# Feed-forward gate and up projections by seven block products, down projections one pair later, modulation weights in smaller pieces

## What is computed

```python
gate, up = split(rmsnorm(x, ffn_norm) @ w_gu)          # w_gu: 1024 x (2 * 2816)
x = x + (silu(gate) * up) @ w_down                     # w_down: 2816 x 1024
c_act = silu(c)
shift, scale, g = split(c_act @ ada_w[l] + ada_b[l])   # l = 0, 1: each 1024 x 3072
shift, scale = split(c_act @ kv_ada_w + kv_ada_b)      # 1024 x 2048
```

## Time and profile before

| | us |
|---|---|
| median of 3 runs | 2555.91 (2554.61 to 2556.51) |
| the profiled execution | 2559.54 |
| its span in the trace | 2557.7 |
| PE busy in the span | 2462.2 (96%) |
| DVE busy | 1272.4 (50%) |
| POOL busy | 1133.5 (44%) |
| ACT busy | 604.0 (24%) |

### The profile page before, as it was taken

One profiled execution on the slowest core, in us unless ns is written; L12 is line 12 of the kernel. 1 busy time (PEld: TensorE's weight loads), 2 busy tenths in 40 slices (PEclk: granted clock), 3 DMA queues, 4 the chain that ended last, 5 costly groups with the idle time before them and its releaser, 6 DMA issues.

```text
span 2557.7 us, 30787 instructions
## 1 busy us (share of the span) xinstructions
PE 2462.2 (96%) x12078; PEld 2040.9 (80%) x12086; DVE 1272.4 (50%) x1519; ACT 604.0 (24%) x1197; POOL 1133.5 (44%) x519
## 2 busy tenths in 40 slices
PE   6999999999999999999999989999999999999987
PEld 5787788887877888888888877888888787888876
DVE  6337555625563444435352677352524465055665
ACT  3111545512430000000000332010110123155532
POOL 5534755034033444444444434444444443555455
PEclk9999999999999999999999999999999999999998
DMA  5511000021011323232321101111111113100033
GB/s 182 162 44 50 1 1 22 13 107 42 17 42 59 132 99 131 85 136 82 148 82 50 49 26 57 42 50 50 49 49 49 41 49 129 45 26 19 25 116 115
DMA packets 45935, 170.97 MB, mean 67 GB/s; under 512 B 4590, under 2 KB 9456, under 8 KB 40456
## 3 DMA queue, kind: packets, MB, share of 16 engines
q1 hardware_dynamic: 37832, 148.52, 16.6%
q10 hardware_dynamic: 8000, 21.01, 2.4%
HBM read 156.90 MB, written 12.57 MB: 66 GB/s over the span
## 4 chain that ended last, share of the span: by engine, by line
PE 87%; DVE 8%; ACT 2%; issue 2%; POOL 1%; DMA 0%; ACTq 0%; DVEq 0%; SPq 0%; POOLq 0%
PE ps L507 24%; PE ps L508 23%; PE ps L510 23%; PE ps L667 5%; PE ps L645 4%; PE ps L655 3%; DVE h_lo L446 1%; DVE sq_sum L350 1%; PE ps L521 1%; PE ps L523 1%; PE ps L522 1%; DVE h_lo L443 1%; DVE pool_b L2359 1%; DVE rms L381 1%; DVE pool_a L2359 0%
## 5 line engine op out<-in xcount | busy, mean ns | idle before, releaser
L1192 POOL TENSOR_TENSOR split_hi<-raw,cf 128x1024 fp32r<-128x1024 f32 x198 | 385.3, 1946 | 1202.2 <-PE ps L510 1099.8
L507 PE MATMUL ps<-h_hi,split_hi 128*128 128x512 f32 x2072 | 830.6, 401 | 36.9 <-issue 9.7
L508 PE MATMUL ps<-h_lo,split_hi 128*128 128x512 f32 x2072 | 812.2, 392 | 0.0
L510 PE MATMUL ps<-h_hi,split_lo 128*128 128x512 f32 x2072 | 664.6, 392 | 0.0
L1194 POOL TENSOR_TENSOR split_lo<-raw,split_hi 128x1024 fp32r<-128x1024 f32 x198 | 557.5, 2816 | 15.5
L507 PEld LDWEIGHTS ps<-h_hi,split_hi 128*128 128x128 f32 x2072 | 392.9, 190 | 124.5 <-issue 18.5
L510 PEld LDWEIGHTS ps<-h_hi,split_lo 128*128 128x128 f32 x2072 | 391.7, 189 | 83.1
L508 PEld LDWEIGHTS ps<-h_lo,split_hi 128*128 128x128 f32 x2072 | 393.0, 190 | 77.2 <-issue 1.7
L507 PE MATMUL ps<-act_hi,split_hi 128*128 128x512 f32 x352 | 138.8, 394 | 3.9 <-DVE act_lo L2278 3.8
L508 PE MATMUL ps<-act_lo,split_hi 128*128 128x512 f32 x352 | 137.6, 391 | 0.0
L655 PE MATMUL ps<-cf,p 128*128 128x128 f32 x712 | 122.6, 277 | 7.4 <-ACT p L797 3.3
(11 more groups left out here) (321 smaller groups left out, 3541.8 us busy)
## 6 DMA issues: line engine op xcount, KB each, us to landing
raw<-in_strips SPq DMA_DIRECT2D x198, 512.0 KB, 3.5
ada_raw<-in_ada SPq DMA_DIRECT2D x32, 1024.0 KB, 5.6
xT<-in_xT SPq DMA_DIRECT2D x4, 1024.0 KB, 7.3
xT<-in_xT ACTq DMA_DIRECT2D x4, 1024.0 KB, 8.5
out_T<-out_sb SPq DMA_DIRECT2D x16, 256.0 KB, 2.2
x_spill_d<-xT ACTq DMA_DIRECT2D x1, 3584.0 KB, 9.9
xT<-x_spill_d ACTq DMA_DIRECT2D x2, 1792.0 KB, 8.6
swa_vec_d<-vbc ACTq DMA_DIRECT2D x1, 3064.0 KB, 19.2
```

The costliest lines, as they stand in the source:

```text
L507: pe.matmul(acc[:, a:b], w_hi, hi[:, a:b], start=first, stop=False)
L508: pe.matmul(acc[:, a:b], w_hi, lo[:, a:b], start=False, stop=False)
L510: mm = pe.matmul(acc[:, a:b], w_lo, hi[:, a:b], start=False, stop=last)
L1192: pool.tensor_tensor(hi, raw[:, r, :], ones[:, 0:1].to_broadcast([P, D]), ALU.mult).then_inc(hi_split, 1)
```

## The change

The first two hidden tiles stay as they were. The 20 others go in ten pairs. For a pair, the gate projection is a block matrix product: 2 hidden tiles x (4 + 4 feature tiles) times (4 + 4 feature tiles) x 2 token halves. It is done in Strassen's way (Winograd's form): seven products of four feature tiles and 512 tokens, 12 matmuls each, instead of eight. The same holds for up. Three of the seven weight blocks are quarters as they are, four are sums or differences of quarters ("form" = a block of 128 x 512 of weights, high and low). The three token-side combinations (`sum_hi`, `sum_lo`) are formed once, during the first two tiles, by DVE (`token_sums`) and ACT (`token_high`).

- POOL forms the block sums and all low parts; ACT makes the high parts (before, POOL made both). Blocks go through four half slots, `FORM_SLOT`. Each pair has 18: 7 gate, 4 down, 7 up.
- PE does a pair's gate quad, then the 8 down products of the pair before, then its up quad; the last pair does gate and up quad and then 8 down products over four hidden tiles. The first product's PSUM result is copied to SBUF by ACT (`first_product`); DVE adds the others in half-width steps to `quad_tmp` and `gated`.
- SP loads the next pair's strip 0 after the 17th block of a pair, strip 1 after the 18th.
- The modulation goes in 8 loop iterations of 8 pieces of 512 KB (128 x 1024) in 2 buffers, with one transpose and reduction each.
- Some semaphores are shared by several events, and the program is built with `dynamic_dma_scratch_size=1024`.

```diff
-HID = 4
-FFN_GROUPS = FFN_TILES // HID
-FFN_REST = FFN_TILES - HID * FFN_GROUPS
+HID = 2
+FFN_ITERS = FFN_TILES // HID - 1
...
 S_CO = S_CQ + 4
 S_FFN = S_CO + 4
-FFN_STRIPS = 3 * HID
-S_FFN_FULL = S_FFN + 3 * FFN_REST
+S_QUADS = S_FFN + 2 * HID
+QUAD_STRIPS = 6
...
+FORMS = 18
+FORM_SLOT = [0, 1, 2, 3, 0, 1, 2, 3, 0, 1, 2, 0, 1, 2, 0, 1, 2, 3]
+FORM_BEFORE = [max(q for q in range(p - FORMS, p) if FORM_SLOT[q % FORMS] == FORM_SLOT[p]) for p in range(FORMS)]
+GATE_AT, DOWN_AT, UP_AT = 0, 7, 11
+LAST_UP_AT, LAST_DOWN_AT = 7, 14
+FORM_BANK = [0, 2, 1, 0, 1, 3, 1]
+QUAD_READS = 7
...
+            def form_low(i, p, src):
+                pool.wait_ge(form_hi, FORMS * i + p + 1)
...
+            def quad_forms(i, e, at, j):
+                form_loaded(pool, i, j)
+                form_loaded(pool, i, j + 1)
+                n = 8 * i + 4 * e
+                pool.tensor_tensor(form_sums[:, :], a21, a22, ALU.add).then_inc(form_sum, 1)
+                pool.wait_ge(form_sum, n + 1)
+                pool.tensor_tensor(a21, a21, a11, ALU.subtract).then_inc(form_sum, 1)
+                for f in range(7):
+                    if f == 2:
+                        form_split(pool, i, at + 1)
+                        pool.tensor_tensor(form_sums[:, :], a11, form_sums[:, :], ALU.subtract).then_inc(form_sum, 1)
+                    if f == 4:
+                        form_split(pool, i, at + 3)
+                        pool.wait_ge(form_sum, n + 3)
+                        pool.tensor_tensor(a12, a12, form_sums[:, :], ALU.add).then_inc(form_sum, 1)
+                    form_low(i, at + f, FORM_SOURCE[f])
...
+            def ffn_pair(i):
+                quad_forms(i, 0, GATE_AT, 0)
+                down_forms(i, DOWN_AT, 2, 4)
+                quad_forms(i, 1, UP_AT, 4)
...
+            def load_quad_strip(i, j, split):
+                if isinstance(i, int) and i == 0 and j < 2:
+                    strip_split(sp, S_QUADS - 2 + j)
+                else:
+                    sp.wait_ge(form_ready, FORMS * i + split)
+                src = dram["strips"][S_QUADS + QUAD_STRIPS * i + j] if isinstance(i, int) else \
+                    dram["strips"][bass.ds(i * QUAD_STRIPS + (S_QUADS + j), 1)].rearrange("a p n -> p (a n)")
+                sp.dma_start(raw[:, j % 2, :], src).then_inc(raw_loaded[j % 2], 16)
+            def ffn_pair(i, ada):
+                load_quad_strip(i, 0, -1)
+                load_quad_strip(i, 1, 0)
+                for k in range(3) if ada else ():
+                    load_ada(i, k)
+                load_quad_strip(i, 2, GATE_AT + 6)
+                load_quad_strip(i, 3, GATE_AT + 7)
+                if ada:
+                    load_ada(i, 3)
+                load_quad_strip(i, 4, DOWN_AT + 2)
+                load_quad_strip(i, 5, DOWN_AT + 4)
+                for k in range(4, 8) if ada else ():
+                    load_ada(i, k)
...
+            def quad(i, e, at):
+                c = 6 * e
+                begin = isinstance(i, int) and i == 0 and e == 0
...
+                    if begin and f < 3:
+                        pe.wait_ge((ffn_gate, ffn_mul, ffn_gate)[f], 2)
+                    elif f < 3:
+                        pe.wait_ge(quad_read, reads + (QUAD_READS * (e - 1) + (2, 5, 7)[f]))
+                    elif f == 3:
+                        pe.wait_ge(quad_first, 2 * i + (e + 1))
+                    else:
+                        pe.wait_ge(quad_read, reads + (QUAD_READS * e + (1, 1, 3)[f - 4]))
+                    if begin and f == 1:
+                        pe.wait_ge(token_sum, 7 * 4)
+                    if begin and f == 6:
+                        pe.wait_ge(token_sum, 7 * 4 + 1)
+                    slot, w = form_at(at + f)
+                    product(pe, bank(FORM_BANK[f]), slot, [(w + k, *form_tokens[f][k]) for k in range(4)], HALF)\
...
+            def down(i):
+                for o in range(8):
+                    if o % 2 == 0:
+                        form_split(pe, i, DOWN_AT + o // 2)
+                    if o == 0:
+                        pe.wait_ge(ffn_lo, HID * i + HID)
+                    if o < 2 and isinstance(i, int):
                         pe.wait_ge(n_ffn["sem"]["root"], n_ffn["done"] + 1)
-                    elif 0 in ks:
-                        pe.wait_ge(ffn_res, o0 + o - 1)
-                    return product(pe, pair(2 + o % 2), (2 * hid + o // tiles) % 2,
-                                   [(hid * (o % tiles) + k, act_hi[:, k, :], act_lo[:, k, :]) for k in ks],
-                                   before=(lambda j: pe.wait_ge(ffn_lo, g0 + ks[j] + 1)) if o == 0 else None,
-                                   start=ks[0] == 0, stop=ks[-1] == hid - 1)
...
+            def quad_high(i, e, at, j, fs):
+                for f in fs:
+                    if f in (0, 6):
+                        form_loaded(act, i, j + (f == 6))
+                    if f in (1, 2, 4, 5):
+                        act.wait_ge(form_sum, 8 * i + (4 * e + {1: 1, 2: 3, 4: 2, 5: 4}[f]))
+                    form_high(i, at + f, FORM_SOURCE[f])
...
+            def first_product(i, e, at):
+                form_through(act, i, at)
+                if e:
+                    act.wait_ge(quad_read, 2 * QUAD_READS * i + QUAD_READS)
+                else:
+                    act.wait_ge(ffn_done, HID * i + HID)
+                act.copy(one_sum, bank(0)).then_inc(quad_first, 1)
...
+            def hidden_high(i, hi):
+                for j in range(HID):
+                    act.wait_ge(ffn_done, HID * i + (HID + j + 1))
+                    act.copy(hi[:, j, :], gated[:, j, :]).then_inc(ffn_hi, 1)
...
+            def ffn_pair(i):
+                first_product(i, 0, GATE_AT)
+                quad_high(i, 0, GATE_AT, 0, range(4, 7))
+                down_high(i, DOWN_AT, 2, range(4))
+                gate_silu(i + 1)
+                quad_high(i, 1, UP_AT, 4, range(3))
+                first_product(i, 1, UP_AT)
+                quad_high(i, 1, UP_AT, 4, range(3, 7))
+                quad_high(i, 2, FORMS + GATE_AT, QUAD_STRIPS, range(4))
+                hidden_high(i, act_hi)
...
+            def token_sums(k):
+                late = xT[:, k, out_tokens[1]]
+                need(dve, token_sum, 7 * k)
+                dve.tensor_tensor(one_sum, late, xT[:, k, out_tokens[0]], ALU.subtract).then_inc(token_sum, 1)
+                dve.wait_ge(token_sum, 7 * k + 1)
+                dve.wait_ge(token_hi, 4 * k + 1)
+                dve.scalar_tensor_tensor(out=three_sum, in0=one_sum, scalar=col("ffn", k), in1=two_sum,
+                                         op0=ALU.mult, op1=ALU.subtract).then_inc(token_sum, 1)
+                dve.wait_ge(token_sum, 7 * k + 2)
+                dve.scalar_tensor_tensor(out=ada_raw[:, k // 2, (k % 2) * HALF:(k % 2 + 1) * HALF], in0=xT[:, 4 + k, out_tokens[0]],
+                                         scalar=col("ffn", 4 + k), in1=three_sum, op0=ALU.mult, op1=ALU.add).then_inc(token_sum, 1)
+                dve.scalar_tensor_tensor(out=two_sum, in0=late, scalar=col("ffn", k), in1=two_sum,
+                                         op0=ALU.mult, op1=ALU.subtract).then_inc(token_sum, 1)
+                dve.wait_ge(token_hi, 4 * k + 2)
...
+            def two_products(i, e, at):
+                form_through(dve, i, at + 2)
+                dve.wait_ge(quad_first, 2 * i + (e + 1))
+                dve.tensor_tensor(two_sum, one_sum, bank(1), ALU.add).then_inc(quad_read, 1)
...
+            def gate_scale(i, j):
+                dve.wait_ge(ffn_silu, HID * i + (HID + j + 1))
+                dve.tensor_tensor(gated[:, j, :], gated[:, j, :], rms3[:, :], ALU.mult).then_inc(ffn_mul, 1)
...
+            def up_tiles(i, at):
+                dve.wait_ge(ffn_mul, HID * i + 2 * HID)
+                form_through(dve, i, at + 3)
+                dve.tensor_tensor(one_sum, one_sum, bank(0), ALU.add).then_inc(quad_read, 1)
+                read_through(i, 1, 2)
+                dve.tensor_tensor(gated[:, 0, t1], gated[:, 0, t1], one_sum, ALU.mult).then_inc(up_mul, 1)
+                more_products(i, 1, at)
+                dve.wait_ge(up_mul, 2 * i + 1)
...
+            def ffn_pair(i, ada):
+                if ada:
+                    ada_add(i, 0)
+                two_products(i, 0, GATE_AT)
+                if ada:
+                    ada_add(i, 1)
+                gate_tiles(i, GATE_AT)
+                if ada:
+                    ada_add(i, 2)
                 for o in range(8):
-                    st = 2 * hid + o // tiles
-                    if o % tiles == tiles - 1:
-                        strip_through(dve, s0 + st, i, per)
...
+                    if not isinstance(i, int):
...
-            with dve.Fori(0, 4) as i:
-                ffn_group(i, HID, False, True)
-            dve.wait_ge(ada_read, 16)
+                    if o in (0, 2):
+                        gate_scale(i, o // 2)
+                    if ada and o % 2:
```

(10 more changed lines are left out.)

548 lines of the change are left out of this document (355 added, 193 removed).

## The result

The changed kernel is slower: 2564.88 us median of 6 executions (2559.81 to 2567.58), against 2555.40 of before (2554.42 to 2556.51, 6 as well), a ratio of 1.0035 with an interval of 1.0022 to 1.0048. I had forecast 2547.8. The profiled execution took 2562.9 us, 3.4 more than the profiled one of before, with a span of 2560.9. The medians are 9.5 us apart. The rest lies in which executions were profiled: that of before is 4.1 us over the median here (its other executions spread by 2 us here, and by up to 7.5 in the later sessions), that of the change 2.0 us under its own (spread 8 us).

What follows compares the result with a forecast made beforehand. PE, fed without pause, was taken as the bound: -54.4 us of matmuls, +14.4, +17.2, -5.4, +12.2, +5.9 and +2.0 for waits and edges gave -8.1, and 3.6 off for the median: 2547.8 us, own range 2536 to 2560.

Steps and rivals of the forecast that it cites:

- Bound and saving: Feed-forward part: PE has no pause; 240 matmuls fewer at 0.2267 us each save 54.4 us.
- (a): Pair boundary: the next pair's strips and POOL's three operations come late, nine times 1.6 us, +14.4 us.
- late next: Uncounted risks: ACT's down copies behind copies waiting for POOL's sums; modulation pieces ahead of strip 0 on SP's queue.
- all waits of (a) to (c) I put under the second: PE clock: each of these waits stays below the 2.43 us idle that was followed by eight matmuls at 0.43 us.
- (c): Third down product waits for the first's residual addition on DVE: 1.2 us, eight times.
- rival 2: Waits at each pair pass the clock's edge and slow matmuls follow: 2576 us, slower; chance 0.25.
- The limit of 4.7 us a pair: Waits in a pair at which the change turns slower than before; the forecast had 3.7 us.
- a pair of 63 to 65 us: Sign: time between the same additions of two iterations; outside this range the forecast is wrong.
- (b): Gate quad's fifth product waits for DVE's first sum: 0.95 us, eight times.
- The price of a meeting: DVE operations with two SBUF inputs and POOL operations stretch one another: 0.95 us a meeting, POOL's taking 1.28 alone.
- (d): First two tiles: the old wait goes, -5.4 us; DVE's 28 token sums bring two new waits, +12.2 us.
- (e): Last pair's up quad: strips issued closer, 4.3 us late plus 1.6 of slow clock, +5.9 us.

Runs made afterwards that it cites:

- the repeat: The changed kernel run once more, unaltered, against the kernel before: 2561.2 us, ratio 1.0015.

## Why the prediction was wrong

**Bound and saving: right.** The 240 matmuls are gone and PE's pitch is the same; PE's busy time fell.

**(a), the boundary: right in mechanism, too small, and wrong in what it triggers.** "Both are there at 16.1" is the failed step. I took twice a strip's bytes for 5.6 us and nothing else in flight. SP issues two modulation pieces right behind, so strip 1 was there 17.2 us after the up quad's start on average: issued at 10.5 as forecast, 0.4 us later because two loads landed 6.0 us after the first issue even without the pieces, and 0.7 through the pieces. POOL's chain behind it and the meeting took 4.6 us for the 4.7 of the forecast. The pieces were in my list of "late next", as something that could hold SP's queue; that they share the transfer with the strips was not. With 2.5 us of wait instead of 1.6, "all waits of (a) to (c) I put under the second" fell as well: six of nine waits of the profile were of 2.88 us or more, and behind five of them came slow matmuls, 9 us. That is rival 2's mechanism at one wait a pair, and it is about as large as the whole difference between the medians (9.5 us, and 4.4 in the repeat). The limit of 4.7 us a pair that I gave for "slower than before" must be read with the slow matmuls in it; with them the measured waits of (a) to (c) are 36.7 us, 4.3 for each of 8.5 pairs, so the last pair and the edges had a part in it too. The pair took 64.9 us on average where the terms give 64.1 (59.9, 3.75 of waits and 0.5 for the edge). So one of the forecast's own signs, a pair of 63 to 65 us, was met by luck: too much at the boundary and too little at (b) and (c). The other, matmuls every 0.43 us, showed that it was wrong.

**(b) and (c): too large.** 17.2 us forecast, 5.3 measured. They aren't independent of (a): a boundary that is 2.9 us late gives DVE as much time to catch up, and in those pairs there was no wait at the fifth gate product at all (928.96 aside). A boundary of 1.47 us was followed by one of 0.9, which is the size that I had worked out. The run with the pieces ahead of the strips shows it the other way round: shorter boundary waits, and 7.0 us at the fifth gate product. The three should have been told as one sum with a maximum, not as three terms.

**The price of a meeting: right, how often they bind not.** L1320 took 1.255 us at its shortest and 1.30 in the median (1.28 taken; the Trainium skill's estimate of 1.11, "GPSIMD Engine Reference", section 3.1, is not borne out). DVE's act_lo took 2.21 in the median (2.18 taken). But DVE was busy 48.5 us a pair where I had 42 and 12 of stretch, and with seven of its 17 two-input operations a pair left out in effect the time fell by 5.5 us only, so in the changed kernel meetings with these were not what bound the pair.

**(d), the start: about right in sum**, 11.4 for 12.2, and that by luck: the two waits were 4.6 and 2.5 us for 3.6 and 5.4, the slow matmuls 4.3 for 3.2. No run tested it alone.

**(e), the last pair: right for its own step** (4.01 measured once it stood free, for 4.3) and incomplete: I priced the loads and didn't walk DVE's and ACT's queues behind them. The waits that these queues made were 3.2 and 5.3 us with 2.0 of slow matmuls; moving the work gained 6.5, since the wait of (e) then stood free.

**The kernel's median** moved by 6 us more than the profiled executions. The forecast took off 3.6 us because the profiled execution of before was that far over its median; that of the change turned out to be 2.0 under its own. No run explains this part of the miss.

## What to carry to other kernels

When a change leaves PE less work, write down for every queue (SP's too) what stands in front of the one operation that the next stage needs, and ask of each transfer what else is in flight when it is issued; here 0.7 us of landing time at each of nine boundaries cost 9.6 us, part of it because the wait passed what PE's clock survives. Waits in one loop aren't added: the longest covers the others, and what is won at one comes back at the next until every queue is in the order of need. A table of buffer slots is also an order: each block that waits for a slot holds all that stands behind it on its engine.

## What the runs showed of the hardware

These counts are from the feed-forward part (755 to 1490 us) of the 15 profiles of the change and its variants. Behind 107 waits of PE of 1.20 to 1.67 us the matmuls ran at the full pitch without exception (992.35 to 992.80 above). Of 13 waits of 1.70 to 1.96 us seven were followed by matmuls at the 1.2 GHz level's pitch of 0.43 us, and of 83 longer ones 71 (1188.09 to 1188.94), for 1.4 to 1.9 us of extra time in most cases and 2.0 to 3.0 in the others. The wait of 3.44 us at 928.96 is one of those without. So the edge, which I had between 1.42 and 2.43, lies between 1.67 and 2.0 us for these waits, and which side a wait near it falls on differs from one place and one execution to the next.

It holds for waits that stand apart. Ahead of the part, in the first profile of the change, a wait of 1.82 us was followed by the full pitch, and one of 1.58 us some 3 us behind it by matmuls at 742.09, 742.51 and 742.94:

```profile
738.16 0.50 PE L554 MATMUL ps<-h_hi,split_hi 128*128 128x512 f32 x1 [1.82 <-DVE h_lo L493]
738.50 0.40 PE L555 MATMUL ps<-h_lo,split_hi 128*128 128x512 f32 x1
...
741.49 0.79 PE L554 MATMUL ps<-h_hi,split_hi 128*128 128x512 f32 x1 [1.58 <-DVE h_lo L493]
742.09 0.63 PE L555 MATMUL ps<-h_lo,split_hi 128*128 128x512 f32 x1
```

The first of two loads of 512 KB issued one behind the other landed after 3.5 to 3.6 us in the median, and the second 5.9 to 6.0 us after the first's issue on average where the modulation pieces went ahead of them or waited for them (5.5 to 6.4). With two pieces issued right behind it was 6.7 (5.8 to 7.8). With two pieces still in flight ahead the first landed after 5.9 us and the second after 7.2 in the block shown.
